# Attention values as the stationary operand in two halves of TensorE, and router logits in quarters

## What is computed

```python
s_loc = einsum('brchd,brjkhd->bhrcjk', qg, kg) * scale + bias      # neighbourhood, masked by column
s_ctx = einsum('brchd,bmhd->bhrcm', qg, k_ctx) * scale             # 256 cached context keys
p = softmax(concatenate([s_loc, s_ctx], axis=-1))
out = einsum(p_loc, v_loc) + einsum(p_ctx, v_ctx)                  # then @ w_out, with the other mixers
...
aff = sigmoid(t @ w_router)                                        # 640 tokens x 16 experts
```

## Time and profile before

| | us |
|---|---|
| median of 3 runs (768.79 to 769.06) | 768.82 |
| the profiled execution | 768.03 |
| its span, first to last instruction | 766.2 |
| attention, 217.9 to 293.4 | 75.5 |
| output projection and second norm, 293.4 to 372.1 | 78.7 |
| routing up to the first expert matmul, 372.1 to 402.7 | 30.6 |
| experts, 402.7 to 722.0 | 319.3 |

### The profile page before, as it was taken

The page is one execution under the profiler, slowest core; times in us unless marked ns, Lnnn a source line. Parts: engine busy times, 40 slices in busy tenths (PEclk is TensorE's granted clock), DMA queues, the critical chain, the costliest instruction groups (busy, mean ns, idle before and its releaser), DMA issues.

```text
span 766.2 us, 11652 instructions
## 1 busy us (share of the span) xinstructions
PE 690.8 (90%) x4811; PEld 420.8 (55%) x4811; DVE 227.4 (30%) x502; ACT 160.5 (21%) x333; POOL 151.3 (20%) x187
## 2 busy tenths in 40 slices
PE   0899999989999999999989999999999999999600
PEld 0656547455468886555785455665466556545300
DVE  0510099800333562332484011111011010110157
ACT  4202201111365772121301010101110101011042
POOL 5107930800053530212110000000000000000040
PEclk9999999999999999999999999999999999999955
DMA  9985860992089120380555889999999999984074
GB/s 257 384 274 104 231 219 13 400 311 86 1 293 348 50 111 1 119 320 28 206 207 186 299 302 392 394 419 382 401 408 409 366 416 394 400 335 152 30 277 134
DMA packets 51398, 192.70 MB, mean 252 GB/s; under 512 B 7152, under 2 KB 9449, under 8 KB 46864
## 3 DMA queue, kind: packets, MB, share of 16 engines
q1 hardware_dynamic: 44048, 169.33, 59.7%
q0 software_dynamic: 7184, 22.57, 8.9%
q10 hardware_dynamic: 112, 0.04, 0.0%
HBM read 169.81 MB, written 22.17 MB: 251 GB/s over the span
## 4 chain that ended last, share of the span: by engine, by line
PE 82%; DMA 7%; DVE 5%; SPq 2%; ACT 2%; issue 1%; POOL 0%; DVEq 0%; POOLq 0%; ACTq 0%
PE bank L1673 13%; PE bank L1680 9%; PE bank L1541 9%; PE bank L1422 7%; PE bank L1696 6%; PE bank L1705 5%; PE bank L1482 4%; PE bank L1369 4%; PE bank L1583 4%; DMA slots<-in_w_ada 3%; PE bank L1385 3%; PE bank L1688 3%; PE bank L1427 2%; PE bank L1660 2%; DMA x<-in_x_prompt 2%; PE bank L1440 2%
## 5 line engine op out<-in xcount | busy, mean ns | idle before, releaser
L1422 PE MATMUL bank<-ra,slots 128*128 128x512 f32 x192 | 83.3, 594 | 0.4 <-DVE ra L813 0.4
L1541 PE MATMUL bank<-slots,rc 128*128 128x512 f32 x160 | 70.4, 594 | 0.0
L1422 PEld LDWEIGHTS bank<-ra,slots 128*128 128x128 f32 x192 | 36.1, 190 | 45.6 <-issue 44.6
L1119 DVE TENSOR_TENSOR rc<-re,bank 128x256 f32<-128x256 f32 (+1 forms) x34 | 10.9, 363 | 169.1 <-PE bank L1680 88.2
L1313 POOL COPY gi<-ridx 128x1 uint32<-128x1 uint32 x19 | 3.5, 185 | 279.4 <-PE bank L1660 245.1
L1673 PE MATMUL bank<-rb,rc 128*128 128x512 f32 x128 | 55.9, 594 | 0.0
L828 DVE SCALAR_TENSOR_TENSOR re<-re,cwT 128x670 f32<-128x670 f32 x60 | 52.3, 950 | 0.0
L537 ACT ACTIVATE rb<-bank 128x512 f32<-128x512 f32 (+1 forms) x64 | 31.1, 525 | 94.7 <-PE bank L1422 49.7
L1541 PEld LDWEIGHTS bank<-slots,rc 128*128 128x128 f32 x160 | 29.7, 190 | 34.0 <-issue 34.0
L1680 PE MATMUL bank<-slots,rc 128*64 128x256 f32 x384 | 43.4, 381 | 0.0
L1201 POOL TENSOR_TENSOR mod<-mod,vecT 128x8 f32<-128x8 f32 (+1 forms) x8 | 19.7, 2457 | 114.3 <-ACT mod L537 114.3
(11 more groups left out here) (274 smaller groups left out, 1010.7 us busy)
## 6 DMA issues: line engine op xcount, KB each, us to landing
slots<-in_w_ada SPq DMA_DIRECT2D x12, 2048.0 KB, 11.8
slots<-in_moe_w_gate SPq DMA_DIRECT2D x9, 2048.0 KB, 11.0
slots<-in_moe_w_up SPq DMA_DIRECT2D x9, 2048.0 KB, 11.7
slots<-in_moe_w_down SPq DMA_DIRECT2D x9, 2048.0 KB, 10.5
rb<-in_moe_w_gate SPq DMA_DIRECT2D x8, 2048.0 KB, 10.7
rb<-in_moe_w_up SPq DMA_DIRECT2D x8, 2048.0 KB, 13.2
rb<-in_moe_w_down SPq DMA_DIRECT2D x8, 2048.0 KB
slots<-in_w_in SPq DMA_DIRECT2D x4, 2048.0 KB, 13.5
```

What stands on the lines that cost most here:

```text
L1422: ins = mm(b[:, :], w[:, k, m * P:(m + 1) * P], hT[:, k, 0:NLAT], start=k == 0, stop=k == KD - 1)
L1541: ins = mm(b[:, :], mT[:, k, i * P:(i + 1) * P], wo[k // 4][:, k % 4, 512 * hf:512 * hf + 512], start=k == 0, stop=k == KD - 1)
```

## The change

Attention now goes by pairs of heads (`PAIRS` = 16, 19 steps). The values are stationary, 64 columns for each head of the pair, one head in columns 0 to 63 of the array and one in 64 to 127, and the turned weights move, 128 columns at a time. The product comes out with the channels on the partitions, as the output projection wants it. The column of ones is gone: the sum of the weights comes from the exponential, which is now one instruction of 512 elements out of PSUM with an accumulated output (DVE writes the biased scores back into the bank). For each tile DVE spreads the eight inverse sums to 128x512 (`spread`), PE turns that block into a bank `R` (four transposes in place of `aT`), and DVE copies `R` out and multiplies (`weigh`). In a step PE does scores, the `BESIDE` work, the values of the pair two steps back, and last the transposes of the pair one step back. ACT's order in a step is stated apart from PE's, as `TAKEN`: first it copies out the `PT`s of this step, then come the two exponentials.

The router's logits of tiles 0 to 3 are made in one go after the last piece of `wo`, with `w_router` stationary in four quarters of 32 columns and the tokens of one tile moving in each (32 matmuls); the result is copied out, turned, and gets one sigmoid. The last tile's eight matmuls run in the four quarters by turns, and a matmul with `fold` adds the quarters. POOL's store of the modulation rows moves to `s == 27` and its four loads to `s == 30`; two small memsets for the ones go, and the constants grow by 16 columns.

```diff
-    for i in range(STEPS):
-        if i < PAIRS and i % 2 == 0:
-            plan += [(("S", i), "A"), (("S", i + 1), "A")]
-        if i in BESIDE:
-            plan.append((BESIDE[i], "D" if BESIDE[i][0] in ("Sc", "wo") else "A"))
-        if 2 <= i < PAIRS + 2:
-            plan.append((("PT", i - 2), "A"))
+    for j in range(STEPS):
+        scores = [(("S", 2 * j + u), "A") for u in range(2) if j < PAIRS]
+        turned = [(("PT", 2 * j - 2 + u), "A") for u in range(2) if 1 <= j < PAIRS + 1]
+        others = [(key, "D" if key[0] in ("Sc", "wo") else "A") for key in BESIDE.get(j, ())]
+        plan += turned + scores + others if evacuation else scores + others + turned
+        if j >= 5 and j % 4 == 1:
+            plan.append((("R", j // 4 - 1), "D"))
...
+BESIDE = {0: [("pw", 0)], 1: [("pw", 1)], 2: [("pwc",), ("ada", 9)], 4: [("adT", 9), ("ada", 10)],
+          6: [("adT", 10), ("ada", 11)], 8: [("adT", 11)], 13: [("modT",)], PAIRS + 1: [("Sc", 0), ("Sc", 1)],
+          PAIRS + 2: [("wo", 0, 0)]}
...
+            for s in (2 * j - 2, 2 * j - 1) if 1 <= j < PAIRS + 1 else ():
+                ge(act, "pv_done", j - 1)
+                b = filled(act, "PT", s)
+                evac(pts[:, s % 2, :], b[:, :])
+            for u in (2 * j, 2 * j + 1) if j < PAIRS else ():
                 act.wait_ge(S["smax_done"], u + 1)
                 b = filled(act, "S", u)
-                nmx = st[:, 2, u:u + 1]
-                sc.activation(pr[:, u % 4, 0:256], pr[:, u % 4, 0:256], ACT.Exp, bias=nmx)
-                evac(pr[:, u % 4, 256:512], b[:, 256:512], ACT.Exp, bias=nmx)
...
+                evac(pr[:, u % 4, :], b[:, :], ACT.Exp, bias=st[:, 2, u:u + 1], accum_out=st[:, 0, u:u + 1])
...
-                for q in range(4):
-                    ins = mm(ob[:, 65 * (h % 4):65 * (h % 4) + 65], pts[:, s % 2, q * P:(q + 1) * P], vals[q],
...
+            for q in range(4):
+                for u in range(2):
+                    h = 2 * m + u
+                    v = (vl[:, tile, h, 0:DH], vl[:, (tile + 1) % 4, h, 0:DH], vc[:, 0, h, 0:DH], vc[:, 1, h, 0:DH])[q]
+                    ins = mm(bank[6 + tile % 2][64 * u:64 * u + 64, m * P:(m + 1) * P], v, pts[:, u, q * P:(q + 1) * P],
...
+            for k in range(KD):
+                for q in (k % 4,) if last else range(4):
+                    tok = slice((TT - 1) * P, TT * P) if last else slice(q * P, (q + 1) * P)
+                    ins = mm(b[32 * q:32 * q + 32, 0:P], wrb[:, k * NE:k * NE + 32], h2T[:, k, tok],
...
```

More of the change, by code:

```diff
@@ L1548, in aT, with score @@
         def aT(i):
-            pe.wait_ge(S["o_free"], 2 * i + 2)
+            pe.wait_ge(S["o_free"], 2)
             transposes(("aT", i), [at[:, m * P:(m + 1) * P] for m in range(4)])
-        def o_bank(u):
-            if u >= 2:
-                pe.wait_ge(S["o_free"], u - 1)
-            return bank[6 + u % 2]
+        def score(pair):
+            tile, m = pair // 4, pair % 4
+            rows = [slice(64 * u, 64 * u + 64) for u in range(2)]
+            b = [take("S", 2 * pair + u) for u in range(2)]
+            for u, p in enumerate(rows):
+                mm(b[u][:, 0:256], qT[p, m, tile * P:(tile + 1) * P], kT[p, m, tile * P:tile * P + 256],
+                   start=True, stop=True)
+            for u, p in enumerate(rows):
+                give(mm(b[u][:, 256:512], qT[p, m, tile * P:(tile + 1) * P], kcT[p, m, :],
+                        start=True, stop=True))
@@ new lines, in values @@
+        def values(pair):
+            tile, m = pair // 4, pair % 4
+            if m == 0 and tile >= 2:
+                emptied(pe, "R", tile - 2)
+            for u in range(2):
+                emptied(pe, "PT", 2 * pair + u)
+            for q in range(4):
+                for u in range(2):
+                    h = 2 * m + u
+                    v = (vl[:, tile, h, 0:DH], vl[:, (tile + 1) % 4, h, 0:DH], vc[:, 0, h, 0:DH], vc[:, 1, h, 0:DH])[q]
+                    ins = mm(bank[6 + tile % 2][64 * u:64 * u + 64, m * P:(m + 1) * P], v, pts[:, u, q * P:(q + 1) * P],
+                             start=q == 0, stop=q == 3)
+            ins.then_inc(S["pv_done"], 1)
@@ new lines, in _ @@
+        for j in range(STEPS):
+            if j < PAIRS:
+                score(j)
+            for key in BESIDE.get(j, ()):
+                beside[key[0]](*key[1:])
+            if 2 <= j < PAIRS + 2:
+                values(j - 2)
+            for s in (2 * j - 2, 2 * j - 1) if 1 <= j < PAIRS + 1 else ():
+                emptied(pe, "S", s)
+                transposes(("PT", s), [pr[:, s % 4, q * P:(q + 1) * P] for q in range(4)])
+            if j >= 5 and j % 4 == 1:
+                pe.wait_ge(S["spread_ready"], j // 4)
+                transposes(("R", j // 4 - 1), [at[:, m * P:(m + 1) * P] for m in range(4)])
@@ L1594, in _ @@
             emptied(pe, "PTc", j)
[L1595 removed]
+            emptied(pe, "R", 2 + j)
+            ob = bank[6 + j]
             for q in range(4):
```

216 lines of the change are left out of this document (99 added, 117 removed).

## The result

The changed kernel takes 776.0 us (median of 4 runs, 774.4 to 776.9) where the kernel before took 768.9 beside it: 1.0091 times, 95% interval 1.0075 to 1.0107. It is slower by 7.1 us. The forecast was slower by 2.8 (771.6, range 766 to 776): the right side, and at the very edge of the range. That it still lies inside is partly luck: the same kernel took 777.0 when it was run again, where the kernel before takes 770.0 (experiment 3), and what lifts it over the forecast is a clock that the sum left out. The profiled execution of after took 776.89, its span is 775.1.

What follows compares the result with a forecast made beforehand. PE was taken to bound attention and output projection. Attention +5.7 (17.0 of waits less 11.3 of work), router -3.5 and routing's end +0.6 gave +2.8 us on the median of 768.82: 771.6 us, range 766 to 776.

Steps and rivals of the forecast that it cites:

- PE bound, less work: In attention, PE is the limit and a pair of heads takes 3.07 in place of 3.78: 11.3 us less work.
- The waits: In attention, PE waits for ring banks that ACT's exponentials empty late: 17.0 us together, 0.07 idle before.
- The exponential: In attention, ACT's exponential of 512 elements with bias and accumulator read was put at 0.79 us.
- Router: In the projection stage, logits of tiles 0 and 1 no longer stand between projections: 3.5 us saved.
- the ranking's +0.6: At the end of routing, a longer chain with a bare table load lets DVE start the last ranking 0.6 us later.
- Rival (d), the clock: In attention, 17 us of waits let the clock fall to 1.2 GHz for a third of the stage: 790, chance 0.03.
- The stretch ahead: From the start to the first score of attention, the forecast difference was 0.
- The range: For the whole kernel, 766 to 776 us at 0.80; kind ends 767.5, unkind ends 775 with half of the excess.

Runs made afterwards that it cites:

- experiment 3: The changed kernel with eight dummy matmuls ahead of the scores of steps 3, 5 and 7: 772.1 us, 1.0033 times before; the changed kernel again, unaltered: 777.0 us.
- experiment 2: The changed kernel with side work and `R` in idle result banks: 764.6 us; also with side work last in each step and matmuls ahead of `ada` 7: 756.2 us.
- experiment 1: The kernel before with the change's router logits alone: 767.2 us, 0.9968 times before; the changed kernel with the router logits of before: 779.8 us, 1.0136.

## Why the prediction was right, and where it was short

- **PE bound, less work.** Right. The trace gave 1.02 for the values. If 0.08 of it is the switch, as eight transposes show it (0.94 when `adT` follows, 233.62 to 234.56, and 1.02 when scores do, 283.82 to 284.84), 0.94 is left for the 0.90; the pair came to 3.11 for 3.07. In experiment 3, where the clock is 1.00, attention is 81.98 - 75.30 = +6.7 where +5.7 was forecast. With 16.5 of waits PE's work seems to have fallen by 9.8 and not 11.3, but a bracket counts only from the modelled end of the last matmul, about 0.07 after PE can take the next (1.09 against 1.02), which is some 0.9 for the 13 waits. In experiment 2, with few waits, the work fell by 11.1 (7.7 in the stage and 3.4 of waits). Known misses are 0.6 for the pair and 0.5 for the turned `R` of tile 3, whose counterpart `aT` stood in the projection before, so that the projection gained it.
- **The waits.** Right almost place by place: behind two more uses of the ring 2.23 (2.34 foreseen), behind one 1.50 and 1.56 (1.55), behind `R` 1.12 (1.11), after step 13 1.79 (1.9), in step 16 0.89 (0.9). The exponential was mis-sized: I put 0.79 to the next, and it is 0.66 (248.20 to 248.86 above), since the accumulator read overlaps as well. It shows little in the waits: the second read ends at 249.65 and PE starts 0.15 later, where I had 0.04 for the wake. That the waits ate the gain is shown by experiment 2: without them attention is 67.6.
- **Router.** Right for the logits between projections. The whole stretch gave -3.5 (experiment 1) where -3.5 and +0.6 were forecast, and -4.0 in after with the moved `aT`: the ranking's +0.6 was +0.3, and +0.1 at the experts.
- **Rival (d), the clock: the step that failed.** I gave it 0.03, on the ground that the waits are "1 to 2.4 us each with dense work between", and priced only a fall for a third of the stage. It came in part, behind the waits of 2.23 and 1.79: 3.1 to 6.3 us in the attention of the changed kernel. The forecast's own sum should have held it as a term.
- **The stretch ahead** was taken as equal. The first score comes between 216.9 and 221.8 in the traces of the changed attention, 217.7 and 221.7 in those of the old one, and the before of the first chip happened to keep its clock there.
- **The range.** Its upper sum does not follow from its own words: 9.4 - 3.5 + 1.3 on 768.8 is 776.0, and half of the excess over the forecast is 773.8, not 775.

With the clock and the stretch ahead, 2.8 + 1.0 (attention's work and waits) - 1.1 (router, `aT`) + 3.1 + 3.3 gives 9.1, the difference at the experts between the two profiled executions.

## What to carry to other kernels

When a change shortens the busiest engine, count the uses that each step puts on a shared ring: one or two extra ones decide whether the next step asks for a buffer of this step or of an earlier one, and a bank that stands idle in turns can take them. Put small side work behind as much work as the copy of its predecessor needs. Compare traces stage by stage, each from its own start, as landing times ahead can hide or fake what a change did.

## What the runs showed that I had not expected

- The granted clock fell behind waits of 2.23 and 1.79 us in attention in some traces and not in others, with the same code and the same wait (1.98 and 1.09 for the values of step 3), at 1.5 to 1.6 us a place, and behind the wait for `ada` 7 in six of the eight traces without matmuls in it.
- Work that nobody needs, placed in a wait, makes the kernel faster: 24 dummy matmuls in three waits of attention brought their clock back, 1.5 to 1.6 us for each that had been slow.
- Half-width products cost 1.02 a pair when the halves alternate and 1.52 when each does its four products in a row, not twice as much.
